# Neighbour attention: the scores of two query tiles in one visit of TensorE, behind the weighing

## The reference

```python
def _na(q, k, v, q_w, k_w, rel_bias, meta_bias):
    ...
    q = _rmsnorm(q.reshape(B, L, NA_HEADS, NA_HEAD_DIM), q_w)
    k = _rmsnorm(k.reshape(B, L, NA_HEADS, NA_HEAD_DIM), k_w)
    ...
        s_win = (jnp.einsum('bqhd,brqchd->bhqrc', q_row, k_win).astype(jnp.float32) * scale
                 + bias.astype(jnp.float32)[None])
        s_meta = jnp.einsum('bqhd,bmhd->bhqm', q_row, k_meta).astype(jnp.float32) * scale + meta_b
        s = jnp.concatenate([s_win.reshape(B, NA_HEADS, GRID_W, n_win), s_meta], axis=-1)
        p = jax.nn.softmax(s, axis=-1).astype(v.dtype)
        ...
        return (jnp.einsum('bhqrc,brqchd->bqhd', p_win, v_win)
                + jnp.einsum('bhqm,bmhd->bqhd', p_meta, v_meta))
```

## Time and profile before

| what | us |
|---|---|
| median of 3 runs | 1289.39 |
| lowest, highest run | 1288.01, 2118.7 |
| span of the profiled execution | 1288.1 |
| TensorE busy in the span | 1267.2 |
| VectorE busy | 729.3 |
| ScalarE busy | 470.9 |
| GpSimd busy | 625.4 |

### The profile page before, as it was taken

How to read it: one execution, slowest core, us unless ns; L and a number is a source line. 1 busy time by engine, 2 the same in 40 slices (tenths; PEclk the granted TensorE clock), 3 DMA queues, 4 the chain that set the end, 5 groups by cost and what they waited for, 6 DMA issues and landing times.

```text
span 1288.1 us, 20042 instructions
## 1 busy us (share of the span) xinstructions
PE 1267.2 (98%) x6790; PEld 1035.3 (80%) x6790; DVE 729.3 (57%) x1395; ACT 470.9 (37%) x1025; POOL 625.4 (49%) x416
## 2 busy tenths in 40 slices
PE   7999999999999999999999999999999999999998
PEld 6877777778788888888887878888888888888876
DVE  5236777567774545453223788778744655555541
ACT  4233333412322222221112466666501555555531
POOL 5423233247454434435664144444437877777722
PEclk9999999999999999999999999999999999999999
DMA  7322222232233332333334211111133332222213
GB/s 204 98 50 83 82 65 67 65 98 85 80 115 97 90 105 81 98 94 90 90 97 121 66 50 50 49 33 49 50 91 100 83 90 79 77 77 78 65 34 98
DMA packets 190611, 105.42 MB, mean 82 GB/s; under 512 B 19174, under 2 KB 186444, under 8 KB 190556
## 3 DMA queue, kind: packets, MB, share of 16 engines
q1 hardware_dynamic: 189748, 102.82, 28.2%
q10 hardware_dynamic: 376, 1.18, 0.2%
q0 software_dynamic: 432, 0.69, 0.2%
HBM read 102.57 MB, written 2.10 MB: 81 GB/s over the span
## 4 chain that ended last, share of the span: by engine, by line
PE 88%; DVE 5%; issue 2%; ACT 2%; POOL 2%; DMA 1%; DVEq 0%; ACTq 0%; POOLq 0%
PE ps L390 20%; PE ps L391 19%; PE ps L392 19%; PE ps L421 8%; PE ps L1521 1%; PE ps L1439 1%; PE ps L1523 1%; PE ps L1522 1%; PE ps L1470 1%; PE ps L1194 1%; PE ps L1450 1%; PE ps L403 1%; PE ps L404 1%; PE ps L407 1%; PE ps L1006 1%
## 5 line engine op out<-in xcount | busy, mean ns | idle before, releaser
L369 POOL TENSOR_TENSOR w_low<-w_raw,w_high 128x1024 fp32r<-128x1024 f32 x180 | 440.3, 2448 | 470.7 <-DVE w_high L364 465.5
L390 PE MATMUL ps<-h_high,w_high 128*128 128x512 f32 x810 | 329.1, 406 | 0.5 <-DVE h_low L530 0.4
L391 PE MATMUL ps<-h_low,w_high 128*128 128x512 f32 x810 | 320.6, 396 | 0.0
L392 PE MATMUL ps<-h_high,w_low 128*128 128x512 f32 x810 | 319.4, 394 | 0.0
L364 DVE CAST w_high<-w_raw 128x1024 fp32r<-128x1024 f32 x183 | 151.8, 831 | 114.0 <-DMA w_raw<-in_w_in_dram 34.8
L390 PEld LDWEIGHTS ps<-h_high,w_high 128*128 128x128 f32 x810 | 152.5, 188 | 39.4 <-issue 5.1
L392 PEld LDWEIGHTS ps<-h_high,w_low 128*128 128x128 f32 x810 | 152.7, 189 | 34.9
L391 PEld LDWEIGHTS ps<-h_low,w_high 128*128 128x128 f32 x810 | 152.6, 188 | 33.5 <-issue 2.4
L1764 ACT ACTIVATE z<-ps,cv 128x512 f32<-128x512 f32 x42 | 32.7, 778 | 147.5 <-PE ps L392 147.5
L2375 DVE SCALAR_TENSOR_TENSOR z<-ps,cv,z 128x511 f32<-128x511 f32 x42 | 31.4, 749 | 91.9 <-ACT z L1764 91.9
L391 PE MATMUL ps<-m_low,w_high 128*128 128x512 f32 x176 | 69.4, 395 | 0.0
(11 more groups left out here) (388 smaller groups left out, 2460.1 us busy)
## 6 DMA issues: line engine op xcount, KB each, us to landing
w_raw<-in_w_in_dram SPq DMA_DIRECT2D x150, 256.0 KB, 3.3
w_raw<-in_w_up_dram SPq DMA_DIRECT2D x88, 256.0 KB, 3.2
w_raw<-in_w_out_dram SPq DMA_DIRECT2D x44, 256.0 KB, 3.0
w_raw<-in_w_down_dram SPq DMA_DIRECT2D x32, 256.0 KB, 3.0
w_raw<-in_w_down_dram SPq DMA_DIRECT2D x16, 192.0 KB, 2.6
rel<-in_rel_bias_dram SPq DMA_DIRECT2D x16, 192.0 KB, 3.7
w_raw<-in_w_ob_dram SPq DMA_DIRECT2D x8, 256.0 KB, 2.8
w_raw<-in_w_oa_dram SPq DMA_DIRECT2D x8, 256.0 KB, 4.1
```

The lines of the kernel that those rows point to most:

```text
L369: pool.tensor_tensor(w_low[:, n % RING, :], w_raw[:, n % RAW, :], w_high[:, n % RING, :].bitcast(F32), ALU.subtract).then_inc(low_made, 1)
L390: pe.matmul(acc, wh, mh, start=first and k == 0, stop=False)
L391: pe.matmul(acc, wh, ml, start=False, stop=False)
L392: done = pe.matmul(acc, wl, mh, start=False, stop=last and k == tiles - 1)
```

## The change

Scores of tiles 0 and 1 are done in one visit, and of tiles 2 and 3 in another; both tiles lie beside each other in the one bank of their head (NA_COL). Each visit stands directly behind a weighing. The first visit of a pair is in that pair, no longer at the end of the one before. The orders of TensorE, ScalarE and VectorE are rewritten for this, the last pair gets functions of its own, ON_CUT is cut anew, and two parts of the output product go in front of the last weighing. VectorE waits once for both tiles of a visit. GpSimd's and SP's code stays. In the diff the removed lines of the old pair functions are left out, as they stand above.

```diff
--- before.py
+++ after.py
@@ -71,9 +71,11 @@
 GATE_BANK = [6, 7, 4, 5]
 OM_BANK = [7, 5, 2, 3, 0, 1, 4, 7]
 
-ON_CUT = [[(0, 0, 0), (0, 0, 1), (0, 1, 0)], [(0, 1, 1), (1, 0, 0), (1, 0, 1)], [(1, 1, 0), (1, 1, 1), (2, 0, 0)],
-          [(2, 0, 1), (2, 1, 0), (2, 1, 1)], [(0, 2, 0), (0, 2, 1), (1, 2, 0)], [(1, 2, 1), (2, 2, 0), (2, 2, 1)],
-          [(3, 0, 0), (3, 1, 0)], [(3, 2, 0)]]
+NA_COL = [0, NA_W[0], 0, NA_W[2]]
+
+ON_CUT = [[(0, 0, 0), (0, 0, 1)], [(0, 1, 0), (0, 1, 1), (1, 0, 0), (1, 0, 1), (1, 1, 0), (1, 1, 1)],
+          [(2, 0, 0), (2, 0, 1)], [(2, 1, 0), (2, 1, 1)],
+          [(0, 2, 0), (0, 2, 1), (1, 2, 0), (1, 2, 1), (2, 2, 0), (2, 2, 1)], [(3, 0, 0), (3, 1, 0), (3, 2, 0)]]
 MASK_COLS = 7 * P
 
 
@@ -1425,19 +1427,21 @@
 
             pe.wait_ge(s["om_added"], 2)
 
-            def scores(i, c, t, first=False):
-
-                w, k0 = NA_W[t], NA_K[t]
-                if t == 0:
+            def scores(i, c, p, first=False):
+
+                if p == 0:
                     pe.wait_ge(s["n_low"], i * 4 + (2 * c + 2))
                 if not first:
-                    pe.wait_ge(s["t_masked"], i * 16 + (8 * c + 2 * t))
-                for q_, k_, one_, end in ((nq_high, nk_high, True, False), (nq_high, nk_low, False, False),
-                                          (nq_low, nk_high, False, True)):
-                    for h in range(2):
-                        d = slice(h * HD, (h + 1) * HD)
-                        mm = pe.matmul(ps[:, h, 0:w], q_[d, t * P:(t + 1) * P], k_[d, k0:k0 + w], start=one_, stop=end)
-                mm.then_inc(s["t_scored"], 1)
+                    pe.wait_ge(s["t_masked"], i * 16 + (8 * c + 4 * p))
+                for t in (2 * p, 2 * p + 1):
+                    w, k0, o = NA_W[t], NA_K[t], NA_COL[t]
+                    for q_, k_, one_, end in ((nq_high, nk_high, True, False), (nq_high, nk_low, False, False),
+                                              (nq_low, nk_high, False, True)):
+                        for h in range(2):
+                            d = slice(h * HD, (h + 1) * HD)
+                            mm = pe.matmul(ps[:, h, o:o + w], q_[d, t * P:(t + 1) * P], k_[d, k0:k0 + w],
+                                           start=one_, stop=end)
+                    mm.then_inc(s["t_scored"], 1)
 
             def turn(i, c, t):
                 pe.wait_ge(s["t_probs"], i * 8 + (4 * c + t + 1))
@@ -1526,49 +1530,58 @@
                 for j, t, o in cuts:
                     if (t, o) == (0, 0):
                         pe.wait_ge(low_made, N_ON + j + 1)
+                    if (j, t, o) == (0, 2, 0):
+                        pe.wait_ge(s["g_done"], 8)
+                    if (j, t) == (3, 0):
+                        pe.wait_ge(s["t_low"], 7)
                     if (j, o) == (0, 0):
                         out_rows(0, t)
                     out_part(0, j, t, o)
 
...
+            def pair(i, c, first=False):
+
+                pe.wait_ge(s["nv_ready"], i * 2 + (c + 1))
+                project(i, c + 1, 0, 0)
+                if c:
+                    weigh(i, c - 1, 1)
+                scores(i, c, 0, first)
+                project(i, c + 1, 0, 1)
+                pe.wait_ge(s["g_done"], i * 2 + (c + 1))
+                project(i, c + 1, 1, 0)
+                sums(i, c + 1, 0)
+                turn(i, c, 0)
+                project(i, c + 1, 1, 1)
+                turn(i, c, 1)
+                pe.wait_ge(s["q_root"], i * 8 + (4 * c + 5))
+                project(i, c + 1, 2, 0)
+                weigh(i, c, 0)
+                scores(i, c, 1)
+                sums(i, c + 1, 1)
+                project(i, c + 1, 2, 1)
+                pe.wait_ge(s["q_root"], i * 8 + (4 * c + 7))
+                project(i, c + 1, 3, 0)
+                turn_v(i, c + 1)
+                turn(i, c, 2)
+                project(i, c + 1, 3, 1)
+                turn(i, c, 3)
+
+            def last_pair(i, c):
+                pe.wait_ge(s["nv_ready"], 8)
+                pe.wait_ge(s["t_low"], 6)
+                early(ON_CUT[0])
+                weigh(i, c - 1, 1)
+                scores(i, c, 0)
+                early(ON_CUT[1])
+                turn(i, c, 0)
+                early(ON_CUT[2])
+                turn(i, c, 1)
+                early(ON_CUT[3])
+                weigh(i, c, 0)
+                scores(i, c, 1)
+                early(ON_CUT[4])
+                turn(i, c, 2)
+                early(ON_CUT[5])
+                turn(i, c, 3)
 
             project(0, 0, 0)
             after(pe, "om")
@@ -1580,17 +1593,18 @@
             project(0, 0, 2)
             project(0, 0, 3, 1)
             turn_v(0, 0)
-            scores(0, 0, 0, first=True)
-            pair(0, 0)
+            pair(0, 0, first=True)
             with pe.Fori(0, 3) as i:
                 pair(i, 1)
                 pair(i, 2)
-            pair(3, 1, more=False)
+            last_pair(3, 1)
+            out_rows(0, 3)
+            out_part(0, 0, 3, 0)
+            out_part(0, 0, 3, 1).then_inc(strip_used, 1)
             weigh(3, 1, 1)
 
 
-            out_rows(0, 3)
-            for j in range(3):
+            for j in range(1, 3):
                 out_part(0, j, 3, 0)
                 out_part(0, j, 3, 1).then_inc(strip_used, 1)
             out_part(0, 3, 3, 0)
@@ -2078,36 +2092,40 @@
                 act.activation(y_high[:, bass.ds(i * 2 + c, 1), q], ny[:, q].rearrange("p (o q) -> p o q", o=1),
                                ACT.Copy).then_inc(s["t_high"], 1)
 
...
+            def pair(i, c):
+                expo(i, c, 0)
                 expo(i, c, 1)
                 if c:
                     y_rounded(i, c - 1)
...
+                square(i, c + 1, 0)
+                copy_a(i, c, 0)
+                root_ln(i, c + 1, 0)
+                root_exp(i, c + 1, 0)
                 copy_a(i, c, 1)
...
+                square(i, c + 1, 1)
                 expo(i, c, 2)
...
+                root_ln(i, c + 1, 1)
+                expo(i, c, 3)
+                root_exp(i, c + 1, 1)
+                high_of(i, c + 1, 0)
+                keep_v(i, c + 1)
+                high_of(i, c + 1, 1)
                 copy_a(i, c, 2)
...
+                place_v(i, c + 1)
+                copy_a(i, c, 3)
+                gate(i, c + 1)
+
+            def last_pair(i, c):
+                expo(i, c, 0)
+                expo(i, c, 1)
+                y_rounded(i, c - 1)
+                copy_a(i, c, 0)
+                copy_a(i, c, 1)
+                expo(i, c, 2)
                 expo(i, c, 3)
...
+                y_rounded(i, c, slice(0, 2 * P))
+                copy_a(i, c, 2)
                 copy_a(i, c, 3)
...
 
             square(0, 0, 0)
             root_ln(0, 0, 0)
@@ -2665,10 +2682,11 @@
                 w = NA_W[t]
                 if t == 0:
                     dve.wait_ge(s["nb_ready"], i * 32 + (16 * c + 16))
-                dve.wait_ge(s["t_scored"], i * 8 + (4 * c + t + 1))
+                if t % 2 == 0:
+                    dve.wait_ge(s["t_scored"], i * 8 + (4 * c + t + 2))
                 dve.memset(nm[:, t % 2, 4, :], 0.0)
                 for h in range(2):
-                    dve.tensor_tensor_reduce(ne[:, t % 2, h, 0:w], ps[:, h, 0:w],
+                    dve.tensor_tensor_reduce(ne[:, t % 2, h, 0:w], ps[:, h, NA_COL[t]:NA_COL[t] + w],
                                              nb[:, c % 2, h, NA_OFF[t]:NA_OFF[t] + w], 1.0, -3e38, ALU.add, ALU.max,
                                              nm[:, t % 2, 3, h:h + 1]).then_inc(s["t_masked"], 1)
 
@@ -2726,38 +2744,49 @@
                 dve.wait_ge(s["g_part"], i * 6 + (3 * c + 3))
                 dve.tensor_tensor(ng[:, c % 2, :], ps[:, 7 if c else 4, :], ng[:, c % 2, :], ALU.mult).then_inc(s["g_done"], 1)
 
...
+            def pair(i, c):
                 ahead = N_NA + 4 * (c + 2)
                 gate(i, c)
                 if c:
                     gated(i, c - 1, 1)
+                masked(i, c, 0)
                 masked(i, c, 1)
+                probs(i, c, 0)
+                keep(i, c + 1, 0)
+                make_high(dve, ahead, i * 8)
+                probs(i, c, 1)
                 copy_b(i, c, 0)
+                normed(i, c + 1, 0)
+                copy_b(i, c, 1)
+                keep(i, c + 1, 1)
+                make_high(dve, ahead + 1, i * 8)
+                gated(i, c, 0)
+                masked(i, c, 2)
+                masked(i, c, 3)
+                probs(i, c, 2)
+                normed(i, c + 1, 1)
+                probs(i, c, 3)
+                make_high(dve, ahead + 2, i * 8)
+                copy_b(i, c, 2)
+                copy_b(i, c, 3)
+                make_high(dve, ahead + 3, i * 8)
+
+            def last_pair(i, c):
+                gate(i, c)
+                gated(i, c - 1, 1)
+                masked(i, c, 0)
+                masked(i, c, 1)
+                probs(i, c, 0)
                 probs(i, c, 1)
...
+                copy_b(i, c, 0)
```

(49 more changed lines are left out.)

40 lines of the change are left out of this document (removed).

## The result

The median of the changed kernel is 1294.15 us over 6 runs (1293.39 to 1296.98), that of the kernel before 1289.36 over 6. The ratio, taken without the one execution of 2118.7 us, is 1.0034, with a 95% interval of 1.0024 to 1.0045: slower by 4.4 us. I had forecast 1288.0 and at most 1292.5. By the 2% measure it is "same", but the interval leaves out no change.

The account below looks back on a forecast made before the run. TensorE, busy all 32.28 us of a pair, was taken as the bound; its 1.16 saving returns as a stall on GpSimd. Ends of -0.5 give 1287.6 on the profile's scale, 1288.9 on the median's; named 1288.0, range 1281 to 1292.5.

Parts of the forecast that it names:

- the stall at sums0: TensorE, ready at 11.01 us, stands 1.16 before sums0 for GpSimd's squares; the steady pair stays at 32.28.
- Joined visits, 0.88 and 0.90: TensorE's two combined score visits per pair take 0.88 and 0.90 us; bounds for each visit 0.72 and 1.10.
- Rival C: In a joined visit the second tile pays entry and exit again: +1.4 us, 1289.0; chance 0.06.
- TensorE at sums0 at 11.01: TensorE's own work would bring it to sums0 11.01 us into the pair, where it took 12.53.
- GpSimd lets it go at 12.17: GpSimd's chain, from VectorE's high half through strip, table and squares, frees sums0 12.17 us into the pair.
- rival B: GpSimd's bias table stretches above 7.06 us beside VectorE's masks and probs: 1290.4 to 1292.1; chance 0.17.
- The second chain: ScalarE's exponentials, y_rounded and squares, then GpSimd's subtraction, would allow sums0 only at 11.6 us even without the table.
- No cost at turn1: VectorE's probs(1) ends about 14.5 us into the pair, TensorE's turn1 comes at 15.8, so no wait.
- From sums0 to the next pair, 20.11: TensorE's stretch from sums0 to the next pair goes from 19.75 to 20.11 us.
- The tightest cover is turn_v: Behind the second visit ScalarE needs 5.9 us, TensorE comes after 6.3; each 0.1 lost would cost 0.7 in all.
- Ends: First pair -0.4, pair 1 +0.3, steady pairs 6 x 0.0, last pair -0.4: sum -0.5 us.
- sentence on shared SBUF interfaces: Skill's rule that GpSimd and VectorE collide on shared SBUF interfaces; read as possibly stretching GpSimd's table, 7.06 to 7.61 us.

Follow-up runs that it names:

- f3: Changed kernel, but VectorE makes a pair's last high half before the copy behind turn3; 1292.64 us, ratio 1.0018 to the kernel before.
- e2: Changed kernel, but GpSimd writes the bias table's four short meta columns behind the low half of the squares; 1287.21 us, ratio 0.9978 to the kernel before.
- f1: Changed kernel, but ScalarE does the two multiplications of probs(1) and VectorE keeps the reciprocal; 1290.98 us, ratio 1.0002 to the kernel before.
- f2: Changed kernel, but GpSimd makes the strip's low half in four instructions of 256 columns; 1290.38 us, ratio 0.9999 to the kernel before.
- g2: f4 plus f1's edit (probs(1)'s multiplications on ScalarE); 1285.72 us, ratio 0.9971 to the kernel before.
- f4: Changed kernel with meta columns behind the squares, sums0 behind projection 1, and both engines' second copies moved earlier; 1285.57 us, ratio 0.9963 to the kernel before.
- g1: e2 plus f1's edit (probs(1)'s multiplications on ScalarE); 1288.38 us, ratio 0.9993 to the kernel before.
- g3: f4 plus f2's edit (strip's low half in four instructions); 1285.96 us, ratio 0.9973 to the kernel before.
- e4: Changed kernel with probs(1) before keep and the strip on VectorE, and sums0 behind projection 1's second half; 1287.81 us, ratio 0.9983 to the kernel before.
- e1: Changed kernel, but VectorE does probs(1) before keep and the strip's high half; 1294.99 us, ratio 1.0054 to the kernel before.

## Why the prediction was wrong

Its forecast was a pair in which the stall at sums0 takes back exactly what TensorE saves. Point by point:

- **Joined visits, 0.88 and 0.90.** Right: 0.91 and 0.90. Rival C (1.10) is out. The first step of a visit still takes 0.21 to 0.23 where the later ones take 0.12, so the entry is paid once and not hidden.
- **TensorE at sums0 at 11.01.** Right: the product ahead of it would have been followed at 1109.76, 11.08 into the pair.
- **GpSimd lets it go at 12.17.** Right to 0.01: 12.18. From the table's start to the squares it took 7.09 in this pair and 7.03 to 7.18 in the six, not 7.61, so rival B as I wrote it, a longer table, did not come. f3 and e2 confirm the head and the end of that chain. The second chain is right too: ScalarE's squares end at 10.15 of the pair, forecast 10.2. The 7.61 of pair 1 before, which I took for a longer table, was four meta copies of 1.16 in place of 0.65, with VectorE's cast beside them: again two engines that met.
- **No cost at turn1 ("probs(1), behind keep and a high half, about 14.5, turn1 at 15.8").** This is the step that failed. Turn1 was due at 16.01 of the pair and probs(1) ended at 16.61, 2.1 later than the 14.5, which stands in the prediction without its working. The multiplications took 3.83 beside the strip and the split, where 0.63 is their free length. At 0.63, begun where they were, they would have ended at 13.4 and had a cover of 2.6. The high half before them took 1.78 beside the squares, 1.1 over its free length, but that much was in the trace of before. What the step costs TensorE is 0.66 a pair. f1 and f2 take out this wait and shorten the pair by 0.7.
- **From sums0 to the next pair, 20.11.** It is 20.99. Of the 0.88, 0.66 is the wait at turn1. Another 0.11 is a restart I did not price: behind a wait the first pair of matmuls of sums0 takes 0.35 (1110.86 to 1111.21); in g2, with no wait there, 0.24. The rest, 0.11, is spread.
- **The tightest cover is turn_v.** Wrong place: turn_v never waited. The cover that went was turn1's, 1.3 us by the prediction's own numbers (14.5 and 15.8), and I never asked under what condition the steps ahead of it would take longer.
- **Ends.** About right. The first pair fell from 31.83 to 31.61 (said -0.4), pair 1 rose by 0.66 (said +0.3; the turn1 wait is in it), the last pair gave 0.47 (said 0.4). Six pairs of 0.66 to 0.97 more are 5.3 us; less 0.2 and 0.5 that makes the 4.6 of the span. (The sum's 6 x 0.0 should read 5 x; at nothing a pair it makes no difference.)

The prediction did name the cause, in its sentence on shared SBUF interfaces, and then asked only what it would do to GpSimd. It is GpSimd that held the ports and VectorE that stood. And it looked for the collision where the masks are, though these read PSUM: beside the table they take 0.39 and 0.43, as the masks of the same widths do elsewhere. What needed asking was which VectorE instructions from SBUF to SBUF now begin behind which GpSimd instruction.

Without the turn1 wait the kernel would have come out as forecast, within the noise: f1 and f2 measure 1.0002 and 0.9999. Their pairs of 32.41 to 32.57 are still 0.1 to 0.3 above the 32.28; that is the rest of the 0.88.

## What to carry to other kernels

When a change moves VectorE work, don't price it at its free length. Look up the same line in every place of the trace; if its length varies with the same shape (0.63, 1.19, 1.63 and 3.83 for 272 columns here), find which GpSimd instruction it ends with, and lay both engines' new timelines side by side. A VectorE instruction that starts just behind a long GpSimd one pays for all of it (3.83 us here). Cutting the long one into four cost GpSimd 0.54 us and gave VectorE back 2.2. And a saving on the busiest engine, some 1 us a pair here, is worth nothing while two covers are used up; moving four short copies in GpSimd's queue (e2) was enough to get below the kernel before (0.9978), and f4, which reorders all four engines, came to 0.9963.

## What was unexpected of the hardware

- Each of two VectorE instructions can be held in turn: 3.83 us for two multiplications that need 0.63, the first till the end of the strip (2.40), the second till that of the split (1.36).
- Between GpSimd instructions that follow without a gap VectorE doesn't always get its turn. Beside the bias table's twelve instructions of 0.54 each, the two multiplications of probs(0) took 1.00 to 1.68 us in some pairs, 2.80 to 2.97 in others and 4.05 or 4.06 in one pair each of f4, g1 and g3. Which of them it is changes from pair to pair of one execution. It isn't the place in the table: f2 has 1.33 and 2.97, and f4 has 4.05, all begun 3.89 us behind its start. What decides it is open.
- Of two instructions that start within 0.06 us the later one stands, whichever engine it is on: 1.78 for VectorE's cast in the changed kernel, 1.81 for GpSimd's squares in e4.
- A wait of TensorE can cost more than its length. In e1 it stood for 2.1 us, and 0.8 us after it had resumed the granted clock fell to 0.50, which cost another 1.5. That the wait brought this about is not shown. Waits of up to 1.6 us at sums0 elsewhere in that execution, and of 1.3 in f4 and g1, had no such fall behind them.
